# Ten stages of a transformer on one core: each mixer's last slabs taken one at a time, the modulation's column sums in parts or inside the mixers

## The chip, the core and the metric

The kernel runs on one core of a Trainium2 chip. The metric is the device time of one execution in microseconds (us). Before the change it is 3786.5 us, the median of 3 runs (3773.27 to 3791.08). TensorE is called PE below, its weight loads PEld, VectorE DVE, ScalarE ACT, GpSimd POOL and SyncE SP.

## The reference: what is computed

One sequence of 256 tokens with 1024 channels passes two blocks of two layers each. In the first block a layer is a SwiGLU, a mixer and another SwiGLU, each behind an RMS norm that a condition vector modulates. In the second block a layer is a mixer and a mixture of 64 experts of which each token takes 8, modulated in the same way (the text is cut).

```
def adaln_in(x, g, m, i):
    return rmsnorm(x, g) * (1 + m[:, i, 1][:, None]) + m[:, i, 0][:, None]

# first_block, layer l
m = (silu(c) @ w_mod[l] + b_mod[l]).reshape(bsz, 3, 3, D_MODEL)      # shift, scale, gate for 3 parts
x = x + 0.5 * m[:, 0, 2][:, None] * swiglu(adaln_in(x, norm_g[l, 0], m, 0), ffn_w1[l, 0], ffn_w3[l, 0], ffn_w2[l, 0])
h = adaln_in(x, norm_g[l, 1], m, 1) @ w_in[l]
mix = mixer_ab(h, ...) if l % 2 == 0 else mixer_cd(h, ...)
x = x + m[:, 1, 2][:, None] * (mix @ w_out[l])
x = x + 0.5 * m[:, 2, 2][:, None] * swiglu(adaln_in(x, norm_g[l, 2], m, 2), ffn_w1[l, 1], ffn_w3[l, 1], ffn_w2[l, 1])
```

`mixer_ab` joins windowed attention (with a bias from a table) and a gated convolution of three taps. `mixer_cd` joins dense attention and a long convolution by Fourier transform. The second block's mixer joins differential attention, a convolution of 31 taps with a layer norm, and stick-breaking attention; each is projected, gated by a sigmoid and summed, and the sum is projected again.

## The kernel before

**Stages.** The work is cut into ten stages, s = 0 to 9: SwiGLU, mixer ab, SwiGLU (layer 0), SwiGLU, mixer cd, SwiGLU (layer 1), then mixer, experts, mixer, experts. The four instruction streams PE, ACT, DVE and POOL are written out by hand, each as one function with the stages in order; between them there are only semaphore waits, so an engine's order is the order of its program text. x, the residual, stays on chip as eight tiles of 128 channels by 256 tokens. Beside the views, stage 1 runs from about 287 us to 450, stage 3 from 653, stage 4 from 857, stage 6 from 1242, stage 7 from 1639, stage 8 from 2530 and stage 9 from 2892.

**Slabs.** All weights come in slabs of 1 MB. SP issues their loads in the order of use into a ring of six places (for the experts three more, called far); a load waits until the matmuls that read the place before have ended. A mixer's linears use a slab as it is (L990). A SwiGLU and the experts use a split: ACT copies a half slab rounded (hi, L1521, L1528, L1768), DVE subtracts that from it (lo, L2073, L2077, L2587), and PE makes three matmuls from hi and lo of both sides (L895 to L897). `first_halves` splits the first half slabs of a stage. DVE calls it before it adds the last products of the stage before; where a stage is marked `early`, ACT has done its copies at the end of the stage before too.

**Start of a stage.** The last four products of a stage, of two tiles each, are added to x by DVE (L2066, eight instructions). ACT squares each tile (`norm`), PE sums the squares over the channels with a matrix of ones (L876, recorded as 16 instructions), ACT takes the root, DVE the reciprocal, and then DVE scales h and ACT adds the shift, tile by tile (L1511, L1513). ACT loads a table of its functions (L1495) before the first root. For the scale, DVE needs the modulation. In stages 0, 1, 3, 4 and 6 PE makes its column sums (`sum_mods`, L890) just behind the square sums; for stages 2, 5, 7, 8 and 9 they stand in the mixer ahead, before its output projection.

**Modulation.** c is a column of 1024, w_mod of one stage 1024 by 3072. POOL loads w_mod in pieces of 512 KB into two buffers (L813), twelve of them for 1024 columns; DVE multiplies each by its part of silu(c) and adds up in a tile `macc` or in a part of `work` (`add_mods`, L1943 and L1946, 1.3 us each). PE then sums over the partitions: 24 matmuls with one column of ones, which the records show as 48 instructions, into PSUM bank 3. DVE's `take_mods` waits for all 24, adds b_mod, halves the gate where it must and multiplies the gain. In the mixers of stages 6 and 8 `add_mods` is called in three steps by `MIX2_STEPS`: before the heads' norms, before the rotation, and before the convolution's mean is subtracted (L2344), behind which ACT squares (L1592) and PE sums the variance (L1128).

**Mixers of stages 1 and 4.** PE goes through eight query blocks: scores, the transposes of the probabilities (L1020), the product with the values; while it does so it also makes the last input slabs. DVE makes the convolution's tiles in blocks 6 and 7 of stage 1. In stage 4 PE then transforms z, DVE multiplies the spectra (L2273), PE transforms back (L1097), and DVE finishes the product (L2278). Behind that PE runs `sum_mods(s + 1)` and then the output projection.

**Experts.** In stages 7 and 9 a router (L1218) chooses, then PE walks through 64 experts. 49 in each stage are "gathered": a transposed copy of their tokens only (wide or narrow) goes through the three slabs of the expert. For expert n PE runs the first matmuls (L1301 to L1307), turns the rows for the next (L1288), adds the outputs of n - 2 to the tokens (`scatter`, L1349), then runs `finish(n - 1)`, the second matmul of the expert before (L1336, it reads `hidden_few` and also waits for DVE's `hg`, L2606, of a later one), and last `turn_few(n)`, the small transpose of its own hidden rows (L1319) from `pre`, which ACT makes (L1812, L1814). The last matmul of `finish` frees the slab.

**Other work in the way.** `more_setup` (two DMAs on ACT's queue, products and an Exp for the second block's lambda and its tables) stands at the end of stage 0's units on ACT and DVE. At stage 6 ACT waits for all eight tiles of x, issues the DMA of the attention masks and then begins its squares.

## Time and profile before

| what | value |
|---|---|
| median of 3 runs | 3786.5 us (3773.27 to 3791.08) |
| the profiled execution's own time | 3798.87 us |
| its span | 3796.9 us |
| PE busy | 3530.8 us, 93% |
| PE weight loads busy | 2989.7 us, 79% |
| DVE busy | 2332.1 us, 61% |
| ACT busy | 1477.7 us, 39% |
| POOL busy | 240.3 us, 6% |
| DMA moved | 842.63 MB, mean 222 GB/s |

The profile is of one execution. Its span is the time from its first to its last instruction. Busy time is the time in which an engine executes; weight loads lie beside matmuls. A matmul counts as busy while it is in PE's pipeline, so 93% is not 93% of PE's peak.

### The profile page before, as it was taken

What the parts mean: (1) busy time and instruction counts of PE and PEld (TensorE: products, weight loads), DVE (VectorE), ACT (ScalarE), POOL (GpSimd) and SP (SyncE); (2) the same over time, 40 slices, a digit from 0 to 9 for tenths busy, and PEclk for the clock granted to TensorE, in tenths of its full rate; (3) what the DMA queues carried; (4) which work ended last, traced back from release to release, by engine and by line L of the source; (5) the groups of instructions that cost most, each with busy time, mean ns of one, the idle gap of its engine ahead of it and who ended that gap; (6) DMA issues with size and microseconds to landing.
All of it is one profiled execution on the core that took longest, in us unless ns stands there. A gap on an engine that the chain in (4) does not pass through costs nothing.

```text
span 3796.9 us, 52579 instructions
## 1 busy us (share of the span) xinstructions
PE 3530.8 (93%) x21065; PEld 2989.7 (79%) x21065; DVE 2332.1 (61%) x3517; ACT 1477.7 (39%) x2212; POOL 240.3 (6%) x337
## 2 busy tenths in 40 slices
PE   4999899999899998889999999999988999999999
PEld 2997799997699787789767676778778976766776
DVE  6774475775377474546666666656554766666666
ACT  1432233432143204133555555541232355555554
POOL 3010010010001000000000000000000000000000
PEclk9999899999899899889999999999998999999999
DMA  7785286784178552345889998875432688898986
GB/s 260 250 297 165 81 293 196 244 293 152 57 245 303 187 188 100 122 153 183 271 283 292 293 286 283 279 239 171 134 121 90 214 273 270 284 289 274 296 274 191
DMA packets 580320, 842.63 MB, mean 222 GB/s; under 512 B 22715, under 2 KB 489760, under 8 KB 578832
## 3 DMA queue, kind: packets, MB, share of 16 engines
q1 hardware_dynamic: 514508, 665.85, 53.5%
q0 software_dynamic: 41056, 147.35, 11.8%
q10 hardware_dynamic: 24548, 26.57, 2.8%
q8 instruction: 140, 2.29, 0.3%
q14 instruction: 68, 0.56, 0.0%
HBM read 836.37 MB, written 3.33 MB: 221 GB/s over the span
## 4 chain that ended last, share of the span: by engine, by line
PE 77%; DVE 9%; DMA 7%; ACT 3%; issue 2%; SPq 1%; DVEq 0%; ACTq 0%
PE bank L990 14%; PE bank L895 11%; PE bank L896 11%; PE bank L897 11%; PE bank L1336 8%; DMA ring<-in_w 3%; DMA far_up<-in_w 3%; PE bank L1349 2%; PE bank L1306 2%; PE bank L1307 2%; PE bank L1203 2%; PE bank L890 2%; PE bank L1301 2%; PE bank L1303 1%; PE bank L1302 1%
## 5 line engine op out<-in xcount | busy, mean ns | idle before, releaser
L897 PE MATMUL bank<-hh,ring_lo 128*128 128x256 f32 (+1 forms) x2176 | 621.7, 286 | 0.0
L895 PE MATMUL bank<-hh,hi 128*128 128x256 f32 (+1 forms) x1984 | 570.8, 288 | 16.7 <-issue 12.3
L896 PE MATMUL bank<-h_lo,hi 128*128 128x256 f32 (+1 forms) x1984 | 567.0, 286 | 0.0
L990 PE MATMUL bank<-h,ring 128*128 128x256 f32 x2432 | 556.4, 389 | 8.4 <-ACT h L1513 8.4
L990 PEld LDWEIGHTS bank<-h,ring 128*128 128x128 f32 x2432 | 475.7, 196 | 80.2 <-issue 12.1
L897 PEld LDWEIGHTS bank<-hh,ring_lo 128*128 128x128 f32 (+1 forms) x2176 | 419.9, 193 | 0.0
L895 PEld LDWEIGHTS bank<-hh,hi 128*128 128x128 f32 (+1 forms) x1984 | 382.7, 193 | 25.3 <-issue 17.6
L896 PEld LDWEIGHTS bank<-h_lo,hi 128*128 128x128 f32 (+1 forms) x1984 | 382.9, 193 | 0.5 <-issue 0.5
L895 PE MATMUL bank<-hid,hi 128*128 128x256 f32 (+1 forms) x1216 | 346.8, 285 | 2.2 <-DVE ring_lo L2592 2.2
L896 PE MATMUL bank<-hid_lo,hi 128*128 128x256 f32 (+1 forms) x1216 | 343.9, 283 | 0.0
L897 PE MATMUL bank<-hid,ring_lo 128*128 128x256 f32 (+1 forms) x1088 | 307.6, 283 | 0.0
L1521 ACT ACTIVATE hi<-ring 128x1024 fp32r<-128x1024 f32 (+1 forms) x184 | 184.0, 1034 | 284.2 <-DMA ring<-in_ffn_w 138.0
L2073 DVE TENSOR_TENSOR ring_lo<-ring,hi 128x1024 fp32r<-128x1024 f32 (+1 forms) x184 | 213.0, 1195 | 109.6 <-ACT hi L1521 109.6
L1336 PE MATMUL bank<-ring,hidden_few 128*64 128x512 f32 (+1 forms) x512 | 242.2, 618 | 40.3 <-DVE hg L2606 40.0
L2587 DVE TENSOR_TENSOR ring_lo<-ring,hi_far 128x1024 fp32r<-128x1024 f32 x176 | 208.5, 1221 | 59.4 <-ACT hi_far L1768 56.5
L895 PEld LDWEIGHTS bank<-hid,hi 128*128 128x128 f32 (+1 forms) x1216 | 233.0, 192 | 3.5 <-issue 2.5
L896 PEld LDWEIGHTS bank<-hid_lo,hi 128*128 128x128 f32 (+1 forms) x1216 | 233.2, 192 | 0.0
L2587 DVE TENSOR_TENSOR ring_lo<-ring,hi 128x1024 fp32r<-128x1024 f32 x168 | 199.4, 1222 | 45.3 <-ACT hi L1768 39.5
L1946 DVE SCALAR_TENSOR_TENSOR macc<-wmod,cond,macc 128x1024 f32<-128x1024 f32 x126 | 160.8, 1281 | 107.5 <-DMA wmod<-in_w_mod 89.4
L813 POOL DMA_DIRECT2D wmod<-in_w_mod x216 | 114.6, 531 | 1713.2 <-DVE macc L1946 985.9
L897 PEld LDWEIGHTS bank<-hid,ring_lo 128*128 128x128 f32 (+1 forms) x1088 | 208.6, 192 | 0.0
L1336 PEld LDWEIGHTS bank<-ring,hidden_few 128*64 128x64 f32 (+1 forms) x512 | 75.5, 157 | 161.6 <-issue 158.3
(372 smaller groups left out, 6642.6 us busy)
## 6 DMA issues: line engine op xcount, KB each, us to landing
ring<-in_w SPq DMA_DIRECT2D x258, 1024.0 KB, 12.3
ring<-in_ffn_w SPq DMA_DIRECT2D x120, 1024.0 KB, 10.5
wmod<-in_w_mod POOLq DMA_DIRECT2D x216, 512.0 KB, 5.6
far_up<-in_w SPq DMA_DIRECT2D x84, 1024.0 KB, 13.1
ring<-in_w_in SPq DMA_DIRECT2D x74, 1024.0 KB, 6.0
work<-in_w SPq DMA_DIRECT2D x42, 1024.0 KB
ring<-in_w_out SPq DMA_DIRECT2D x16, 1024.0 KB, 5.1
ring<-in_w_mod SPq DMA_DIRECT2D x12, 1024.0 KB, 12.7
```

The costliest lines, as they stand in the source:

```text
L813: pool.dma_start(wmod[:, q % 2, :], w[l][k][:, at:at + D]).then_inc(mod_full[q % 2], 16)
L890: ins = pe.matmul(bank[3][:, j:j + 1], mod_sums(n)[:, j * P:(j + 1) * P], M["ones"][:, 0:1], start=True, stop=True)
L895: pe.matmul(o, w_hi, x_hi, start=start, stop=False, skip_group_check=True)
L896: pe.matmul(o, w_hi, x_lo, start=False, stop=False, skip_group_check=True)
L897: return pe.matmul(o, w_lo, x_hi, start=False, stop=stop, skip_group_check=True)
L990: ins = pe.matmul(o[:, half * T:(half + 1) * T], l_, r_, start=(k == 0), stop=(k == KD - 1))
L1203: ins = pe.matmul(bank[4 + j % 4][:, (m % 2) * T:(m % 2 + 1) * T], w[:, k, m * P:(m + 1) * P], src[:, k, :], start=(k == 0), stop=(k == CT ...
L1336: ins = pe.matmul(bank[2 + half][0:m, :], hidden_few[:, c * m:(c + 1) * m], w[:, c, half * 512:(half + 1) * 512], start=(c == 0), stop=(c ...
L1521: act.activation(up_hi(j, t, m), up_half(slots[j], t, m), ACT.Copy).then_inc(hi_done, 1)
L1946: dve.scalar_tensor_tensor(out=acc, in0=w, scalar=c, in1=acc, op0=ALU.mult, op1=ALU.add).then_inc(mod_step, 1)
L2073: dve.tensor_tensor(up_half(slots[j], t, m, ring_lo), up_half(slots[j], t, m), up_hi(j, t, m), ALU.subtract).then_inc(lo_done, 1)
L2587: dve.tensor_tensor(unit_up(slot, True)[:, j, :, c], unit_up(slot)[:, j, :, c], up_hi(j, t, P, n % 2), ALU.subtract).then_inc(lo_done, 1)
```

## The change: what it does

**Banks.** `sum_mods` becomes `sum_columns` with a choice of columns and bank. At the norms of stages 1, 3, 4 and 6 `sum_first` sums the scale into bank 0, the shift into bank 3 and the gate into bank 1, each with its own count on the semaphore; DVE takes scale and shift before it scales h, the gate after the fourth tile (second in stage 3).

**Mixers.** The sums for stages 2 and 5 move ahead of the last block's transpose of stage 1 (bank 5) and ahead of the inverse transform of stage 4 (bank 7). Those of stage 8, made in stage 6's end before, come at the start of stage 7; those of stage 9 are split over two branch projections of stage 8.

**Ends of mixers.** `end_mixer` replaces `next_halves` and `add_out` on ACT and DVE: first half slab split, four tiles added and squared, other half slabs split, last four tiles. PE sums the first four squares ahead of the last output slab.

**Moves.** `more_setup` goes behind stage 1's norm, the masks' DMA behind that and `load_bias`; the ACT wait at the end of stage 2 is taken out, and in stages 2, 3 and 5 the split of the third slab goes behind the norm. `MIX2_STEPS[8]` becomes 8, 6, 6 (the rest of its pieces is added later, as before). With the experts `turn_few(n)` goes ahead of `finish(n - 1)`, on ACT `turned_few(n)` ahead of `out_hi(n - 1)`, on DVE `out_lo` behind the product; `hidden_few` gets two buffers.

```diff
-        hidden_few = nc.alloc_sbuf_tensor_at("hidden_few", [P, T], F32, offset=place["macc"] + 4 * (2 * D + 2 * T))
+        hidden_few = [nc.alloc_sbuf_tensor_at("hidden_few", [P, T], F32, offset=place["macc"] + 4 * (2 * D + 2 * T)), work[:, 64, :]]
...
+        SHIFT, SCALE, GATE, ALL = range(0, KD), range(KD, 2 * KD), range(2 * KD, 3 * KD), range(0, 3 * KD)
+        SUMS = [("all", 0), ("scale", 1), ("shift", 1), ("gate", 1), ("all", 2), ("scale", 3), ("shift", 3), ("gate", 3),
+                ("scale", 4), ("shift", 4), ("gate", 4), ("all", 5), ("scale", 6), ("shift", 6), ("gate", 6), ("all", 7), ("all", 8), ("all", 9)]
...
-        MIX2_STEPS = {6: (12, 6, 6), 8: (8, 4, 4)}
+        MIX2_STEPS = {6: (12, 6, 6), 8: (8, 6, 6)}
...
+            def norm(s, parts=range(KD)):
...
+                for k in parts:
                     pe.wait_ge(sq_done, KD * s + k + 1)
                     ins = pe.matmul(bank[2][:, 0:T], M["ones"], sq[:, (k + 4) % KD, :], start=(k == 0), stop=(k == KD - 1))
-                ins.then_inc(ms_done, 1)
...
+                if KD - 1 in parts:
+                    ins.then_inc(ms_done, 1)
...
+            def sum_columns(n, columns, to, at=0):
...
+                for i, j in enumerate(columns):
+                    ins = pe.matmul(bank[to][:, at + i:at + i + 1], mod_sums(n)[:, j * P:(j + 1) * P], M["ones"][:, 0:1], start=True, stop=True)
+                return ins
+
+            def sum_mods(n, to=3):
...
-                for j in range(MODT):
-                    ins = pe.matmul(bank[3][:, j:j + 1], mod_sums(n)[:, j * P:(j + 1) * P], M["ones"][:, 0:1], start=True, stop=True)
-                ins.then_inc(mod_summed, 1)
+                sum_columns(n, ALL, to).then_inc(mod_summed, 1)
...
+            def sum_first(n):
...
+                pe.wait_ge(mod_step, MOD_STEPS * n)
+                sum_columns(n, SCALE, 0).then_inc(mod_summed, 1)
+                sum_columns(n, SHIFT, 3).then_inc(mod_summed, 1)
+                sum_columns(n, GATE, 1).then_inc(mod_summed, 1)
...
                         linear(slabs[6 + i // 2], 6 + i // 2, taken0, halves=(i % 2,))
+                    if i == 7 and sec["kind"] == "ab":
+                        pe.wait_ge(proj_taken, taken0 + 6)
+                        sum_mods(s + 1, 5)
                     turn_probs(X, i, probs(i))
                     value(i)
                 if sec["kind"] == "cd":
...
                 pe.wait_ge(*X("o_taken", 4))
-                sum_mods(s + 1)
                 pe.wait_ge(*X("conv", CT))
                 for c in range(4):
                     linear(slabs[9 + c], 9 + c, taken0, heads=att)
...
+                    if c == 2:
+                        norm(s + 1, range(4))
...
                     ins.then_inc(X["uf"], 1)
+                sum_mods(s + 1, 7)
                 pe.wait_ge(*X("prod", 4))
...
+                        if (br_, half) == (1, 1) and s == 8:
+                            pe.wait_ge(*X("o_taken", 8))
+                            pe.wait_ge(mod_step, MOD_STEPS * 9)
+                            sum_columns(9, range(0, MODT // 2), 3)
+                        if (br_, half) == (2, 0) and s == 8:
+                            sum_columns(9, range(MODT // 2, MODT), 3, MODT // 2).then_inc(mod_summed, 1)
...
-                sum_mods(8 if s == 6 else 9)
...
                 for c in range(4):
                     linear(slabs[34 + c], 40 + c, taken0)
+                    if c == 2:
+                        norm(s + 1, range(4))
...
+                        turn_few(n)
                         finish(n - 1)
-                        turn_few(n)
...
-                norm(sec["s"])
-                if sec["s"] in (0, 1, 3, 4, 6):
-                    sum_mods(sec["s"])
+                norm(sec["s"], range(4, KD) if sec["behind_mixer"] else range(KD))
+                if sec["s"] in (0, 7):
+                    sum_mods(0 if sec["s"] == 0 else 8)
+                if sec["s"] in (1, 3, 4, 6):
...
+                if not sec["behind_mixer"]:
+                    act.activation(idle, eps, ACT.Sqrt)
+                    squares(s, range(KD))
...
+                if sec["kind"] == "ffn" and sec["early"]:
+                    first_halves(sec, 2)
...
+            def end_mixer(sec):
...
+                act.activation(idle, eps, ACT.Sqrt)
+                split_up(slots[0:1], 0, lambda j: counts[0], m)
+                squares(s, range(4))
+                act.wait_ge(full[slots[1]], counts[1])
+                act.activation(up_hi(1, 0, m), up_half(slots[1], 0, m), ACT.Copy).then_inc(hi_done, 1)
+                first_halves(nxt, 1)
+                if nxt["kind"] == "moe":
+                    first_halves(nxt, 2)
+                squares(s, range(4, KD))
...
-                        act.wait_ge(down_done, tile + 3)
                         first_halves(plan[sec["s"] + 1], 1)
...
+                        turned_few(n)
                         out_hi(n - 1)
-                        turned_few(n)
...
-                if s == 6:
-                    act.wait_ge(x_done, KD * (s + 1))
-                    act.dma_start(masks.rearrange("p a t -> p (a t)"), A["k_causal"]).then_inc(masks_in, 16)
                 norm(sec)
                 if s == 1:
+                    more_setup()
                     load_bias()
+                    act.dma_start(masks.rearrange("p a t -> p (a t)"), A["k_causal"]).then_inc(masks_in, 16)
                 if s == 6:
...
-                dve.wait_ge(mod_summed, s + 1)
-                then(dve.tensor_tensor(m[:, :], bank[3][:, 0:MODT], vec[:, bg, ba:ba + MODT], ALU.add))
-                if s < 6 and s % 3 != 1:
+                m, first, end = modc[:, n % 3, :], columns[0], columns[-1] + 1
+                if what is not None:
+                    dve.wait_ge(*sums(*what))
+                then(dve.tensor_tensor(m[:, first:end], bank[b][:, at:at + end - first], vec[:, bg, ba + first:ba + end], ALU.add))
+                if n < 6 and n % 3 != 1 and end == 3 * KD:
                     then(dve.tensor_scalar(m[:, 2 * KD:], m[:, 2 * KD:], 0.5, None, ALU.mult))
-                then(dve.scalar_tensor_tensor(out=gain[:, s % 3, :], in0=m[:, KD:2 * KD], scalar=1.0, in1=vec[:, gg, ga + row * KD:ga + (row + 1) * KD],
-                                              op0=ALU.add, op1=ALU.mult))
+                if first <= KD < end:
+                    then(dve.scalar_tensor_tensor(out=gain[:, n % 3, :], in0=m[:, KD:2 * KD], scalar=1.0, in1=vec[:, gg, ga + row * KD:ga + (row + 1) * KD],
+                                                  op0=ALU.add, op1=ALU.mult))
...
-                if s not in (7, 8):
-                    take_mods(s)
+                if s == 0:
+                    take_mods(0, ("all", 0), 3)
+                if s in (1, 3, 4, 6):
+                    take_mods(s, ("scale", s), 0, 0, SCALE)
+                    take_mods(s, ("shift", s), 3, 0, SHIFT)
                 dve.wait_ge(rstd_done, s + 1)
                 for k in range(KD):
                     dve.scalar_tensor_tensor(out=h[:, k, :], in0=x[:, k, :], scalar=gain[:, s % 3, k:k + 1], in1=rstd[:, :], op0=ALU.mult, op1=ALU.mult).then_inc(scaled_done, 1)
+                    if s in (1, 3, 4, 6) and k == (1 if s == 3 else 3):
+                        take_mods(s, ("gate", s), 1, 0, GATE)
...
+                    if sec["early"]:
+                        first_halves(sec, 2)
...
                         conv_tile(2 * (i - 6))
+                        if i == 7:
+                            take_mods(s + 1, ("all", s + 1), 5)
                         conv_tile(2 * (i - 6) + 1)
...
+                    take_mods(s + 1, ("all", s + 1), 7)
                     for t in range(CT):
...
+                lo_up(slots[0:1], 0, lambda i: counts[0][0], m)
+                add_out(0)
+                add_out(1)
+                dve.wait_ge(hi_done, counts[0][1])
+                dve.tensor_tensor(up_half(slots[1], 0, m, ring_lo), up_half(slots[1], 0, m), up_hi(1, 0, m), ALU.subtract).then_inc(lo_done, 1)
+                first_halves(nxt, 1)
+                if nxt["kind"] == "moe":
+                    first_halves(nxt, 2)
+                add_out(2)
+                add_out(3)
...
-                        out_lo(n - 1)
                         spread_slots(n)
                         if slots(n) == NARROW:
                             dve.wait_ge(product_done, g0 + p + 1)
-                            dve.tensor_tensor(hidden_few[:, 0:P], product[:, 0:P], bank[1][:, P:2 * P], ALU.mult).then_inc(hid_done, 2)
+                            dve.tensor_tensor(hidden_few[p % 2][:, 0:P], product[:, 0:P], bank[1][:, P:2 * P], ALU.mult).then_inc(hid_done, 2)
+                        out_lo(n - 1)
...
                 norm(sec)
+                if s == 1:
+                    more_setup()
...
                 if sec["kind"] == "moe":
+                    if s == 7:
+                        take_mods(8, ("all", 8), 3)
```

## Rows read from the trace of the kernel before

**Rows 1.** The page, the chain that ended last: shares of the span by engine.

```profile
PE 77%; DVE 9%; DMA 7%; ACT 3%; issue 2%; SPq 1%; DVEq 0%; ACTq 0%
```

**Rows 2.** Timeline, stage 1's start (start us, duration us, engine, line, operation; [idle before, releaser]).

```profile
284.66 3.22 DVE L2066 SCALAR_TENSOR_TENSOR x<-bank,modc,x 128x256 f32<-128x256 f32 x8 [1.98 <-PE bank L897]
...
295.60 5.92 PE L890 MATMUL bank<-mats,work 128*128 128x1 f32 x48
...
303.15 1.19 PE L990 MATMUL bank<-h,ring 128*128 128x256 f32 x2 [1.63 <-ACT h L1513]
...
334.73 3.35 DVE L2175 RECIPROCAL work<-work 128x512 f32<-128x512 f32 x1 [12.38 <-ACT work L1599]
```

**Rows 3.** Timeline, stage 4's start.

```profile
854.66 3.22 DVE L2066 SCALAR_TENSOR_TENSOR x<-bank,modc,x 128x256 f32<-128x256 f32 x8 [1.98 <-PE bank L897]
...
860.08 7.09 PE L890 MATMUL bank<-mats,work 128*128 128x1 f32 x48
...
868.79 1.62 PE L990 MATMUL bank<-h,ring 128*128 128x256 f32 x3 [1.63 <-ACT h L1513]
```

**Rows 4.** Timeline, stage 3's start.

```profile
648.73 1.58 ACT L1521 ACTIVATE hi<-ring 128x768 fp32r<-128x768 f32 x2 [2.50 <-PE bank L897]
...
657.02 5.58 PE L890 MATMUL bank<-mats,macc 128*128 128x1 f32 x48
...
664.91 0.50 PE L895 MATMUL bank<-hh,hi 128*96 128x256 f32 x1 [2.31 <-issue]
```

**Rows 5.** Timeline, stage 6's start.

```profile
1239.61 3.23 DVE L2066 SCALAR_TENSOR_TENSOR x<-bank,modc,x 128x256 f32<-128x256 f32 x8 [1.98 <-PE bank L897]
...
1243.26 1.28 ACT L1495 ACT_TABLE_LOAD   x1 [6.87 <-DVE x L2066]
...
1260.15 1.19 PE L990 MATMUL bank<-h,ring 128*128 128x256 f32 x2 [1.63 <-ACT h L1513]
```

**Rows 6.** Timeline, end of the mixer of stage 1.

```profile
405.77 1.12 PE L1020 MATMUL bank<-mats,pb 128*128 128x128 f32 x4 [2.95 <-DVE pb L2233]
...
410.12 10.40 PE L890 MATMUL bank<-mats,macc 128*128 128x1 f32 x48 [0.47 <-ACT work L1642]
```

**Rows 7.** Timeline, end of the mixer of stage 4.

```profile
991.85 9.53 PE L1097 MATMUL bank<-work 128*128 128x256 f32 x32 [8.39 <-DVE work L2273]
...
1001.21 8.17 PE L890 MATMUL bank<-mats,macc 128*128 128x1 f32 x48
...
1002.77 0.42 DVE L2278 TENSOR_TENSOR h<-work 128x256 f32<-128x256 f32 x1
```

**Rows 8.** Timeline, start of stage 2: the square sums.

```profile
451.21 3.72 PE L876 MATMUL bank<-pb,mats 128*128 128x256 f32 x16 [1.57 <-ACT pb L1499]
```

**Rows 9.** Timeline, end of stage 6 and start of stage 7.

```profile
1602.72 5.76 PE L890 MATMUL bank<-mats,macc 128*128 128x1 f32 x48
...
1646.19 1.09 PE L1218 MATMUL bank<-wr,h 128*128 128x64 f32 x4 [3.51 <-ACT h L1513]
```

**Rows 10.** Timeline, around the layer norm of stages 6 and 8.

```profile
1423.11 2.53 DVE L1946 SCALAR_TENSOR_TENSOR macc<-wmod,cond,macc 128x1024 f32<-128x1024 f32 x2 [4.30 <-DMA wmod<-in_w_mod]
...
1428.12 3.78 PE L1128 MATMUL bank<-work,mats 128*128 128x256 f32 x8 [4.75 <-ACT work L1592]
...
2690.71 1.06 ACT L1592 ACTIVATE work<-work 128x1024 f32<-128x1024 f32 x1 [5.59 <-DVE work L2344]
...
2692.95 1.89 PE L1128 MATMUL bank<-work,mats 128*128 128x256 f32 x8
```

**Rows 11.** Expert stages: a wait (us, times, longest), a chain row, two timeline rows.

```profile
PE bank L1336 <- DVE hg L2606: 50.9, 34, 3.0
...
2216.12 13.05 DMA ring<-in_w
...
2180.09 0.58 ACT L1814 ACTIVATE pre<-bank 128x512 f32<-128x512 f32 x1
...
2181.80 1.10 PE L1319 MATMUL bank<-sort,pre 128*128 128x64 f32 x8
```

95 lines of the change are left out of this document (44 added, 51 removed).

## The prediction

> **What bounds the kernel now.** I read the page first: the shares, then the chain that ended last. TensorE (PE) is 77% of that chain, so a microsecond is won only where PE stands still or does work that could lie in a standstill [rows 1]. Then I took the timeline at the start of every stage (stage s is the code's section s, 0 to 9), at the ends of the four mixers, and the waits of the two expert stages (7 and 9), and asked at each spot which wait ends last. Three kinds show up. At a stage's start PE sums squares, then makes 48 one-column matmuls for the modulation, and only then does the vector engine (DVE) form h: those 48 take 5.6 to 7.1 us there [rows 2 to 4]. At the end of mixers 1 and 4 the same 48 stand between the last attention or convolution work and the output projection, 10.4 and 8.2 us, just behind PE waits [rows 6, 7]. In the expert stages PE waits 50.9 us in 34 places for DVE's hg in front of an expert's second matmul [rows 11].
>
> **Order at stage starts (stages 1, 3, 6).** Stage 4 is the pattern with nothing in the way: first add to x at 854.66, square sums over at 860.08, 5.4 us later, first slab at 868.79, 14.1 us later [rows 3]. In stage 1 the set-up that the diff moves makes this 10.9 us (284.66 to 295.60) [rows 2]: gain 5.5. What it issues (two DMAs, some fifteen small DVE operations, an Exp on ScalarE (ACT) and its table, with one table change back) now lies behind the norm of stage 1, where DVE later waits 12.38 us for ACT's roots while PE runs its first slabs [rows 2]; without that cover it costs about 4 us. In stage 6 ACT waited 6.87 us, until all eight tiles were added, then issued the mask DMA and loaded its table at 1243.26, and only then squared; first add to first slab takes 20.5 us (1239.61 to 1260.15) [rows 5]. By stage 4's 14.1 us the order is worth 6.4. In stage 3 ACT waits 2.50 us for PE before it splits the next slab's second half [rows 4]; with the wait gone and the third slab's split behind the norm, DVE's adds can begin when the sums are there. I take 2.1 of the 2.50.
>
> **Three banks at the norms (stages 1, 3, 4, 6).** Now DVE waits for all 48, then needs three or four operations and ACT one before PE starts: in stage 1 PE starts its slab 7.55 us after the square sums (295.60 to 303.15), of which 5.92 are the 48 [rows 2]; in stage 4 8.71, of which 7.09 [rows 3]; in stage 3 7.89, of which 5.58 [rows 4]. After the change DVE goes on when two thirds are done, and the gate's third runs beside it; but PE is in order, so its slab can't start before all 48 are done. New starts: 5.92 and 7.09 us behind the square sums, so 1.6 us won in each of stages 1 and 4; in stage 3 both paths end near 5.5, so 2.3. And h is then ahead of PE's first half slab, which today gets one tile per 0.4 us: estimate 0.9 more in stages 1, 4 and 6, after the gate's own two small DVE operations are paid. Stage 6 as stage 4 then takes 5.4 + 7.1 = 12.5 us from add to slab, 12.6 with the wait's own cost, so 7.9 less than its 20.5, and 0.9. Totals: stage 1 8.0, stage 3 4.4, stage 4 2.5, stage 6 8.8. The least is the order alone (5.5, 2.1 and 6.4, so 14.0), the most also has the sums at 5.6 us each (3 more).
>
> **Sums into the mixers.** Mixer 1: the 48 move in front of the last transpose, where PE waited 2.95 us; today they take 10.40 at its end [rows 6]. The work is the same, so only the wait is filled: gain 3.0. Behind the new PE operation are the last transpose and value product; DVE's wait for it stands ahead of the last convolution tile, which ends before PE is through. Mixer 4: they go in front of the inverse transform, where PE waits 8.39 us; they took 8.17 [rows 7], so they fit. What is late next: DVE's last product of the convolution, ending at 1003.19 (1002.77 plus 0.42), which the sums hid; PE can then start at about 1003.3 instead of 1009.24: gain 6.0. Below: 3 if the sums slow the matmuls behind; above: 8 with 2.4 GHz throughout.
>
> By the Trainium skill (TensorE: Matmul & The Clock Gate, "The HAM clock gate") activity releases the throttle, so sums laid into waits should run at 2.4 GHz and win more. The trace doesn't bear this out for one-column matmuls: those issued back to back at 410.12 took 10.40 us, those at 1602.72 5.76 [rows 6, 9]. By the page mixer 1 would win 7.6 instead of 3.0, and the whole would come to 3748.
>
> **Slab by slab (stages 2, 5, 7, 9).** In stage 2 DVE did no add before the third slab was split, so all eight adds and squares came behind PE's last slab: PE stood 1.57 us, then made the square sums in 3.72 [rows 8], over 5.3 us after that slab. New: four square sums (half of 3.72, so 1.86) stand in front of it, and behind it remain two adds, two squares and two sums, about 2.0 us: gain 1.4. DVE no longer takes the modulation behind the reciprocal: 0.5 more. Stage 5 repeats stage 2: 4.0 for both. In stages 7 and 9 PE had no wait there; four sums move from behind the slab to ahead of it, between a loss and a gain of one sum pair (0.5), and I take 0. In stage 7 the modulation's 5.76 us [rows 9] leave PE's path to the projection and fall into the 3.51 us that PE waits for h before the router where 2.3 stick out; 0.4 goes to the modulation's DVE operations: gain 3.1. Stage 9's 48 are put between two projections where PE is busy: 0.
>
> **Earlier mod steps in stage 8.** The counts go from 8, 4, 4 to 8, 6, 6. Each step waits for its own 512 KB DMA through two buffers. Two more before the rotation: about 1.6 us of DVE, and the tap chain behind it shifts. Two more before the mean is subtracted: stage 6, which has six there, shows them: the last two came after 4.30 us of waiting and took 2.53, 6.8 together, PE's variance matmul stood idle 4.75 us and took 3.78 us instead of 1.89 [rows 10]. In stage 8 PE had no wait there (2692.95), and ACT's squares were done at 2691.77, 1.2 us before [rows 10]. So 1.6 plus 6.8 minus 1.2 plus about 1.1 for slower matmuls (half of stage 6's excess of 1.9): a loss of 8.3. What it removes (four steps beside projections, no PE wait) wins nothing. Bounds: loss of 4 to 11.
>
> **Experts: the transpose ahead of the second matmul.** Per gathered expert the small transpose (1.10 us for a narrow one [rows 11], 0.4 for a wide one) goes ahead of the previous expert's second matmul, into the hg wait. Counted place by place, each wait filled by at most the transpose, this gives about 29 us over the 98 experts. Against it: the transpose waits for pre, which ACT makes after splitting a slab that may just be landing. At 2180.09 it makes pre while PE is already in the second matmul; PE would have stood 2.5 us there [rows 11]. Such places and small ones of 0.1 to 0.4 sum to some 11 us. And the second matmul's end frees the slab whose loads take 13.05 us on the chain [rows 11]. Counted from the end of one such matmul to another, both orders have the same number of transposes, so a chain that runs over slab loads gets no shorter; only waits inside DVE and ACT count. Ends: minus 11 and plus 29; I take 3, nearest to the chain.
>
> **The sum.** 8.0 + 4.4 + 2.5 + 8.8 + 3.0 + 6.0 + 4.0 + 3.1 - 8.3 + 3.0 = 34.5 us. Against the profiled execution (3798.87 us, span 3796.9) that is 3764.4; that execution is 12.4 above the median of the runs, 3786.5, so I forecast 3752.
>
> **Rivals.**
> *The experts' waits are really filled.* If DVE and ACT, not loads, set the hg waits, the 29 count in full: 3752 - 26 = 3726. For it: the waits end on DVE. Against: behind DVE stand ACT and a 13 us load on the chain. Chance 0.13.
> *Only the orders count.* If PE's in-order queue takes back what the split sums and the mixers' sums fill, there remain 14.0 at three starts, 4.0 in stages 2 and 5, minus 8.3: gain 9.7, 3777. For it: filled waits bring PE no less work. Against: 8.39 us of idle PE with 8.17 us of work to put in. Chance 0.20.
> *Slower: later releases.* Each second matmul of the experts now ends later by the transpose, 66 by 1.1 and 32 by 0.4, 85 us in all. If the loads are what bounds stages 7 and 9, and the transposes don't get ahead of their waits, every delay is passed to a load: 31.5 - 85, so 54 us slower, 3840. It decides from about 40% of these delays on. For it: loads of 13 us on the chain. Against: the same number of transposes on a path between two releases. Chance 0.07.
> The forecast has 0.60, its own range 3740 to 3765.
>
> **Range and chances.** From just under the first rival to the second: 3728 to 3778. A measurement of this kernel tells about 0.5% from no change, 19 us, so from 3767.6 down it is faster: the forecast, the first rival and a little of the second, 0.76; within, 0.17; slower 0.07.
>
> **What would show it.** Right: square sums of stages 1 and 6 end 5.4 us after the first add; stage 1's set-up stands behind its norm without PE waiting; no 48 sums ahead of mixer 1's and 4's projections, and a PE wait of about 2 us for DVE there in mixer 4; in stage 8 a PE wait of 5 to 7 us before the variance matmul and later tap chain; in the experts PE's idle for hg down but new idle for pre, and stages 7 and 9 within 5 us of before. Wrong: hg waits gone and the expert stages over 10 us shorter; no wait in stage 8; or the expert stages longer with loads landing later.

## The result, and the profile after

The changed kernel takes 3742.28 us (median of 4 runs, 3736.55 to 3747.96), the kernel before 3779.92 in the same comparison; the ratio is 0.9893, 95% interval 0.9871 to 0.9915. In a second comparison of the same two programs it is 3740.68 against 3787.87, ratio 0.9868 (0.9848 to 0.9888). So it is faster by 38 us in the one and 47 in the other; 34.5 were forecast. The profiled execution has a span of 3741.5 us, against 3796.9 before, 55.4 less. That pair seems to overstate the gain: the execution of before shown ahead of the prediction took 3798.87 us, where the medians of before are 3779.92 to 3791.28 in the four comparisons (but 3800.03 for the same program as b_again, below).

The page of the changed kernel: span, busy times, chain that ended last.

```profile
span 3741.5 us, 52688 instructions
PE 3523.4 (94%) x21065; PEld 2988.2 (80%) x21065; DVE 2328.0 (62%) x3525; ACT 1464.8 (39%) x2213; POOL 246.2 (7%) x337
PE 75%; DVE 11%; DMA 8%; ACT 4%; issue 2%; SPq 1%; DVEq 0%; ACTq 0%
```

PE is busy for 7.4 us less and idle for 48 less, and DVE's and DMA's share of the chain is up [rows 1]: the gain is PE idle time. Where it was shows a window for each stage, from its first weight matmul to that of the next (stage 9: to PE's last). First the changed kernel, then a second profile of the kernel before. Columns: stretch, length, then busy us (instructions) of PE, PEld, DVE, ACT, POOL; granted clock of PE (1.00 is 2.4 GHz, 0.50 is 1.2), DMA share, GB/s. Length less PE busy is PE's idle time.

```profile
93.33:295.57 202.24, 202.24 (x1648) 201.82 (x1649) 148.00 (x192) 79.72 (x105) 19.01 (x36) 0.98 0.78 268
295.57:447.42 151.85, 139.78 (x632) 119.80 (x632) 64.24 (x138) 38.98 (x91) 6.41 (x12) 0.91 0.40 131
447.42:650.48 203.06, 202.03 (x1649) 201.56 (x1649) 140.06 (x187) 82.64 (x108) 12.66 (x24) 0.98 0.70 237
650.48:852.51 202.03, 202.03 (x1649) 201.61 (x1649) 148.93 (x193) 80.62 (x106) 19.00 (x36) 0.98 0.77 265
852.51:1024.28 171.77, 151.16 (x661) 124.06 (x662) 84.46 (x149) 35.94 (x82) 6.33 (x12) 0.92 0.32 103
1024.28:1226.20 201.92, 201.92 (x1648) 201.50 (x1649) 148.84 (x193) 80.52 (x106) 19.01 (x36) 0.98 0.80 273
1226.20:1605.34 379.14, 346.18 (x1542) 294.71 (x1542) 210.92 (x395) 91.42 (x159) 17.94 (x34) 0.95 0.43 145
1605.34:2486.80 881.46, 847.54 (x5005) 665.97 (x5006) 562.40 (x816) 438.03 (x643) 53.25 (x51) 0.98 0.84 267
2486.80:2859.80 373.00, 341.24 (x1492) 288.68 (x1493) 191.79 (x371) 86.74 (x152) 12.76 (x24) 0.95 0.40 133
2859.80:3737.09 877.29, 845.15 (x5004) 663.54 (x5004) 562.11 (x818) 434.78 (x635) 48.82 (x49) 0.99 0.82 261
```

```profile
99.73:308.06 208.33, 202.83 (x1649) 201.77 (x1649) 149.01 (x209) 79.49 (x105) 19.00 (x36) 0.98 0.77 261
308.06:464.31 156.25, 139.33 (x630) 118.95 (x631) 63.12 (x121) 38.24 (x92) 6.41 (x12) 0.90 0.41 132
464.31:669.84 205.53, 201.32 (x1648) 200.61 (x1649) 139.73 (x185) 82.85 (x108) 12.67 (x24) 0.98 0.68 227
669.84:873.72 203.88, 202.25 (x1648) 201.78 (x1649) 147.14 (x190) 78.81 (x103) 19.01 (x36) 0.98 0.78 263
873.72:1054.26 180.54, 152.47 (x660) 125.16 (x661) 85.73 (x151) 37.88 (x86) 6.34 (x12) 0.90 0.34 106
1054.26:1265.14 210.88, 205.86 (x1648) 204.69 (x1649) 147.14 (x190) 77.83 (x103) 19.01 (x36) 0.96 0.76 257
1265.14:1648.85 383.71, 351.46 (x1541) 298.30 (x1541) 209.54 (x393) 90.58 (x157) 17.94 (x34) 0.93 0.43 143
1648.85:2538.09 889.24, 845.39 (x5004) 663.67 (x5005) 567.91 (x819) 446.80 (x648) 50.16 (x51) 0.98 0.83 265
2538.09:2893.96 355.87, 330.99 (x1493) 283.38 (x1493) 191.36 (x371) 86.87 (x152) 12.76 (x24) 0.97 0.43 139
2893.96:3783.43 889.47, 846.11 (x5004) 664.90 (x5004) 565.81 (x818) 440.60 (x635) 45.24 (x49) 0.98 0.81 257
```

Stages 0, 3 and 5 now have no idle PE at all from one first slab to the next: length and busy time are equal. Stage 8 is the one that became longer. The timeline of the changed kernel at the starts of stages 1 and 6 and at the sums of stages 3 and 4, which answers to [rows 2 to 5]:

```profile
282.55 3.23 DVE L2119 SCALAR_TENSOR_TENSOR x<-bank,modc,x 128x256 f32<-128x256 f32 x8 [1.97 <-PE bank L914]
287.96 7.75 PE L891 MATMUL bank<-mats,work 128*128 128x1 f32 x48
295.57 1.20 PE L1007 MATMUL bank<-h,ring 128*128 128x256 f32 x2
...
642.30 7.15 PE L891 MATMUL bank<-mats,macc 128*128 128x1 f32 x48
...
846.26 6.39 PE L891 MATMUL bank<-mats,work 128*128 128x1 f32 x48
...
1213.76 3.23 DVE L2119 SCALAR_TENSOR_TENSOR x<-bank,modc,x 128x256 f32<-128x256 f32 x8 [1.98 <-PE bank L914]
1219.17 7.17 PE L891 MATMUL bank<-mats,work 128*128 128x1 f32 x48
1226.20 2.05 PE L1007 MATMUL bank<-h,ring 128*128 128x256 f32 x4
```

At the starts of stages 1 and 6 the sums begin 5.4 us after the first add, and the first slab starts when they end, with no wait. Stage 1's now take 7.75 us instead of 5.92, stage 3's 7.15 instead of 5.58, stage 4's 6.39 instead of 7.09. The mixers, stage 8's layer norm and the projection of stage 6, answering to [rows 6, 7, 9, 10]:

```profile
395.40 10.24 PE L891 MATMUL bank<-mats,macc 128*128 128x1 f32 x48
...
975.43 4.97 PE L1119 MATMUL bank<-work 128*128 128x256 f32 x11 [1.11 <-DVE work L2329]
...
986.87 3.62 PE L1007 MATMUL bank<-work,ring 128*128 128x256 f32 x8 [1.93 <-issue]
...
1566.51 22.67 PE L1007 MATMUL bank<-h,ring 128*128 128x256 f32 x96 [1.96 <-DVE h L2513]
...
2648.09 3.78 PE L1150 MATMUL bank<-work,mats 128*128 128x256 f32 x8 [5.58 <-ACT work L1641]
```

Mixer 4's wait of 8.39 us is down to 1.11. Before its output projection a new wait of 1.93 us stands: the profile names no releaser, but DVE's last product of the convolution ends at 986.77, 0.1 us before the projection starts, as the prediction had it. The projection of stage 6, which followed the sums, now waits 1.96 us for the merged h. Stage 8's variance matmul waits 5.58 us and takes 3.78 instead of 1.89. And PE's waits in the experts, answering to [rows 11] (us in total, times, longest), first of the changed kernel, then of the changed kernel with the old order of the experts (a_noswap, below):

```profile
PE bank L1366 <- DVE hg L2674: 14.2, 23, 0.9
PE bank L1349 <- ACT pre L1863: 8.6, 10, 3.0
PE bank L1345 <- DVE product L2710: 5.7, 14, 0.7
```

```profile
PE bank L1366 <- DVE hg L2674: 51.7, 33, 3.6
```

### The profile page after: what moved, and what is told of

Same layout as the page of the kernel before. It is cut to its first block, busy times and chain, and to the rows that moved or that the text cites. A ratio compares the mean times of both kernels' runs of the same rounds, so it can differ in the third digit from the quotient of the medians.

```text
span 3741.5 us, 52688 instructions
## 1 busy us (share of the span) xinstructions
PE 3523.4 (94%) x21065; PEld 2988.2 (80%) x21065; DVE 2328.0 (62%) x3525; ACT 1464.8 (39%) x2213; POOL 246.2 (7%) x337
## 3 DMA queue, kind: packets, MB, share of 16 engines
q0 software_dynamic: 41056, 147.35, 11.7%
## 4 chain that ended last, share of the span: by engine, by line
PE 75%; DVE 11%; DMA 8%; ACT 4%; issue 2%; SPq 1%; DVEq 0%; ACTq 0%
PE bank L1007 12%; PE bank L912 11%; PE bank L914 11%; PE bank L913 11%; PE bank L1366 8%; DMA ring<-in_w 3%; DMA far_up<-in_w 3%; DVE work L2400 2%; PE bank L1335 2%; PE bank L1379 2%; PE bank L1336 2%; PE bank L1231 2%; PE bank L1330 2%; PE bank L891 1%; PE bank L1331 1%
## 5 line engine op out<-in xcount | busy, mean ns | idle before, releaser
L1559 ACT ACTIVATE hi<-ring 128x1024 fp32r<-128x1024 f32 (+1 forms) x180 | 180.5, 1035 | 110.2 <-DMA ring<-in_ffn_w 84.4
L795 POOL DMA_INDIRECT got<-rows_scratch,slot_tok x98 | 98.5, 1005 | 1700.4 <-PE bank L1317 1258.2
L1817 ACT ACTIVATE hi_far<-ring 128x1024 fp32r<-128x1024 f32 x176 | 178.2, 1057 | 66.1 <-DMA ring<-in_w 66.1
## 6 DMA issues: line engine op xcount, KB each, us to landing
ring<-in_w_mod SPq DMA_DIRECT2D x12, 1024.0 KB, 12.1
```

What stands on the lines that cost most here:

```text
L795: pool.indirect_dma_start(got[0:m, p % 2, :], None, rows_dram[l].ap(), bass.IndirectOffsetOnAxis(slot_tok[0:m, rank - WIDE_FROM:rank - WID ...
L1559: act.activation(up_hi(j, t, m), up_half(slots[j], t, m), ACT.Copy).then_inc(hi_done, 1)
L1817: act.activation(up_hi(j, t, P, n % 2), unit_up(slot)[:, j, :, t * P:(t + 1) * P], ACT.Copy).then_inc(hi_done, 1)
```

## The experiments

All ratios are to the kernel before, of the same comparison.

**b_again**: no edit.

> The kernel before, unchanged. The two profiled executions differ by 55.4 us, the medians by 37.6, so either the profiled execution of before was a long one (its 3798.87 us against a median of 3780) or the changed one a short one. If the first, this profile has a span near 3780 and its stages 7 and 9 (first matmul to first matmul 891.3 and about 898 us before) are shorter by most of the difference, since DMA is what varies; the PE wait for hg in them is then nearer 40 us than the 50.9 of before. If the waits are the kernel's own, hg stays at 51 us within 2. The ratio shows what the measurement can tell: 1.000 within 0.003.

3800.03 us, ratio 1.0013 (0.9996 to 1.0031); span 3787.8. Stages 7 and 9 together have 1778.7 us against 1784.7 in the first profile, stage 8 355.9 against 361.7, stages 0 to 5 the same within 0.1. The first profile was long by 11.8 us in these three stages. The hg waits are 46.9 us, between the two expectations. That DMA is what varies is not shown: the 5.8 us of stage 8 are all PE busy time (336.8 against 331.0, at a granted clock of 0.96 and 0.97), and of the 6.0 in stages 7 and 9 only 4.2 are PE idle time.

**b_swap** and **a_noswap**: the experts' order alone, and everything but it.

```diff
-                        finish(n - 1)
-                        turn_few(n)
+                        turn_few(n)
+                        finish(n - 1)
```
(ACT and DVE likewise; b_swap has two `hidden_few` too.)

> The kernel before with the experts' order alone: the small transpose ahead of the second matmul, two buffers for the hidden rows, the outputs' splits behind. My forecast (loads set the pace, the filled waits come back elsewhere): 3 us faster, within 5. The rival (PE sets the pace, what the waits lose is won): 20 to 29 us faster, as the profiled pair has it: stages 7 and 9 shorter by 26 us there with hg waits 36.7 us less and 14.3 us of new waits for pre and product. If the pair overstates it by the long execution of before, about 10 to 18.

> The changed kernel with the experts' three orders put back (PE, ACT and DVE; the second buffer stays). By my forecast 3 us slower than the changed kernel, 3745; by the rival 20 to 29 us slower, 3762 to 3771, with hg waits of PE back at about 50 us. With the kernel before with the swap alone it tells whether the gain is additive.

b_swap: 3777.89 us, ratio 0.9958 (0.9940 to 0.9977), so 16 us faster. a_noswap: 3758.89, ratio 0.9918 (0.9903 to 0.9933), 9 us more than the changed kernel's 0.9893 in the first comparison and 19 more than its 0.9868 in the second. The lengths of stages 7 and 9 together, in all profiles but that of a_pre844:

```
old order: 1784.7 1778.7 1781.6 1782.5                              mean 1781.9, PE idle 89.7
new order: 1773.7 1758.8 1767.1 1770.0 1768.5 1773.1 1771.7 1760.4 1772.0   mean 1768.4, PE idle 69.5
```

The two sets don't overlap; the swap is worth 13.5 us. PE idles 20.2 us less, and 6.7 of them come back as longer PE busy time. My forecast of 3 is wrong, and the rival's 20 to 29 is too high: 29 is twice what came. The 16 us of b_swap, whose profile stands for one execution only, fit the third expectation, 10 to 18.

**b_orders**: `more_setup` and the masks' DMA moved, nothing else.

```diff
-                if s == 6:
-                    act.wait_ge(x_done, KD * (s + 1))
-                    act.dma_start(masks...)
                 norm(sec)
                 if s == 1:
+                    more_setup()
                     load_bias()
+                    act.dma_start(masks...)
```
(`more_setup` is taken from the end of stage 0 on both engines; DVE calls it behind stage 1's norm likewise.)

> The kernel before with two moves alone: more_setup behind stage 1's norm, the masks' DMA behind stage 1's norm instead of ahead of stage 6's squares. Forecast by the prediction's terms: stage 0 to the first slab of stage 1 5.5 us shorter (208.3 to 202.8), stage 5 to the first slab of stage 6 6.4 shorter (210.9 to 204.5), nothing lost in stage 1 (156.2): 11.9 us in all, 0.9969. Rival: the moved set-up holds DVE and ACT where the queries' norms need them, stage 1 is 2 to 4 us longer.

3777.45 us, ratio 0.9961 (0.9945 to 0.9978): 15 us, where 11.9 were forecast. The profiled execution was the longest of 13, and its granted clock was lower in most stages (0.93 in stages 0, 3 and 5 where others have 0.98; 0.90 in stage 8), so its windows of stages 0, 1 and 5 are read with care:

```profile
97.79:301.92 204.13, 202.50 (x1649) 201.93 (x1649) 147.76 (x190) 78.60 (x103) 19.01 (x36) 0.93 0.78 266
301.92:462.47 160.55, 143.82 (x630) 120.41 (x631) 65.36 (x140) 40.91 (x95) 6.43 (x12) 0.87 0.41 131
1049.87:1253.38 203.51, 201.88 (x1649) 201.32 (x1649) 147.20 (x190) 78.59 (x103) 19.01 (x36) 0.93 0.78 265
```

Even so stages 0 and 5 are 4.2 and 7.4 us shorter than before (5.5 and 6.4 were forecast). Stage 1 is 4.3 longer, but its idle time (length less busy) is 16.7 us against 16.9 before: PE's busy time is 4.5 longer at 0.87, and the moved set-up added no wait. The rival falls.

**a_again**: the changed kernel a second time.

> The changed kernel, unchanged, beside the others of this call: the base from which they are read. The profiles so far have stages 0 to 5 of the changed kernel within 1 us of each other but for stage 1 (146.1, 150.9 and 151.9 us), and the expert stages spread over 13 us and more for one and the same order. Expected: ratio to before 0.988 to 0.991, stages 7 and 9 together near 1770 us, between the 1760.4 of the first profile and the 1773.3 of the kernel with 8, 4, 4. If the first profile's 1760.4 comes again, the experts' order is worth over 20 us; if 1770 and more, about 10.

3740.68 us, ratio 0.9868. Stages 7 and 9: 1767.1. Stage 1 took 146.1 us instead of 151.9 with the same program.

**a_wait48**: DVE waits for the gate's sums, the last third, before scale and shift.

```diff
-                    take_mods(s, ("scale", s), 0, 0, SCALE)
-                    take_mods(s, ("shift", s), 3, 0, SHIFT)
+                    take_mods(s, ("gate", s), 0, 0, SCALE)
+                    take_mods(s, ("gate", s), 3, 0, SHIFT)
```

> The changed kernel, but DVE waits for all 48 column sums at the norms of stages 1, 3, 4 and 6 before it takes scale and shift; banks and PE's order stay. By the prediction's terms the split wait is worth 2.5, 2.3, 2.5 and 2.4 us there, 9.7 in all, which would come back: 3752. The rival after the first comparison: stage 0 gained 6.1 us of which the order alone explains 5.5, so the split wait is worth about 0.6 in stages 1 and 6 and the sums themselves have become longer (7.75 us instead of 5.92 in stage 1): 2 to 5 us come back.

3757.02 us, ratio 0.9905 (0.9884 to 0.9926), 14 us more than a_again. Its windows of stages 0, 2, 3 and 5:

```profile
97.72:301.85 204.13, 202.32 (x1649) 201.84 (x1649) 147.22 (x191) 78.80 (x103) 19.08 (x36) 0.98 0.78 266
453.01:657.72 204.71, 202.28 (x1648) 201.81 (x1649) 140.23 (x187) 82.77 (x108) 12.72 (x24) 0.98 0.70 235
657.72:861.83 204.11, 202.30 (x1649) 201.82 (x1649) 148.46 (x192) 79.70 (x104) 19.08 (x36) 0.98 0.78 263
1035.11:1239.11 204.00, 202.19 (x1648) 201.71 (x1649) 148.57 (x192) 79.62 (x104) 19.08 (x36) 0.98 0.79 270
```

They are 2.0, 1.8, 2.1 and 2.1 us longer than in a_again, 8.0 together, and 1.8, 1.4, 1.8 and 1.8 of it is new PE idle time. So the split wait is worth 8.0 where the prediction had 9.7; the rival's 2 to 5 is refuted. The other 6 of the 14 us I can't place: in the profile stage 1 is 5.1 us longer too, but all of that is PE busy time at a lower clock (0.92 against 0.95), which differs between executions of one program.

**a_oldends**: the mixers' ends in the old order.

```diff
-                    if c == 2:
-                        norm(s + 1, range(4))
...
+                first_halves(nxt, 0)
+                first_halves(nxt, 1)
+                act.activation(idle, eps, ACT.Sqrt)
+                squares(s, range(KD))
```

> The changed kernel with the ends of the mixers as before: all half slabs of the next stage split first, then the eight adds, all squares and square sums behind the last slab. By the prediction 4.0 us slower, 2.0 each at the starts of stages 2 and 5 (stage 1 and stage 4 longer by that) and nothing in 7 and 9. Rival: the early square sums also help stages 7 and 9, by 1 to 2 us each, because PE then waits for the last squares there, or they hurt by delaying the last slab's products.

3743.00 us, ratio 0.9862 (0.9838 to 0.9886) against 0.9868: no difference, but an interval of 9 us to either side could not show 4. The windows of stages 1 and 4 can:

```profile
300.07:445.64 145.57, 133.67 (x631) 114.67 (x632) 64.14 (x138) 38.93 (x91) 6.40 (x12) 0.95 0.43 139
850.35:1021.64 171.29, 149.98 (x662) 122.08 (x662) 84.44 (x149) 35.89 (x82) 6.33 (x12) 0.91 0.34 106
```

0.5 and 0.8 us shorter than in a_again. Both expectations are wrong for these stages. From the end of stage 1's last slab to the first matmul of stage 2 the old order takes 7.6 us (438.05 to 445.64) and the changed kernel 6.3 (441.12 to 447.42), but that one has made four square sums in 1.7 us ahead of the slab. Before it was 9.9 (449.5 to 459.35). Of the 2.3 us between before and the old order 0.4 are the modulation, which DVE no longer takes behind the reciprocal (in a_mixback, where it does, the gap is 6.75 us instead of 6.30). Most of the rest is PE's wait for the first squares, 1.57 us in before and none in a_oldends. In before DVE began its adds at 450.23, when it had split the third slab (1.22 us from 449.09; ACT's copy for it had waited for the slab's load); in both later kernels that split stands behind the norm. No run moves the split alone.

**a_mixback**: sums for stages 2 and 5 back at the mixers' ends.

```diff
                 pe.wait_ge(*X("o_taken", 4))
+                sum_mods(s + 1)
                 pe.wait_ge(*X("conv", CT))
```
(and out of their new places; DVE takes them behind the reciprocal.)

> The changed kernel with the sums for stages 2 and 5 back at the ends of the mixers of stages 1 and 4. By the prediction 9.0 us slower (3.0 in stage 1, 6.0 in stage 4): stage 1 at 149 to 155 us, stage 4 at 178. The whole gain of stages 1 and 4 over before (4.3 to 10.1 and 7.5 to 8.7) must then be of these moves, since the old ends cost nothing. Rival: part of it comes from the modulation no longer being taken behind the reciprocal (0.5 us each) and from the clock, which stands at 1.2 GHz during the sums in some executions and at 2.4 in others; then stage 1 comes out anywhere between 146 and 156.

3767.63 us, ratio 0.9936 (0.9915 to 0.9957), 26 us more than a_again, and 16 more than the changed kernel's first comparison; its profile, against a_again's, shows 17 us in stages 1 and 4:

```profile
301.60:457.66 156.06, 139.34 (x632) 119.24 (x632) 64.00 (x138) 38.96 (x91) 6.41 (x12) 0.92 0.40 128
862.95:1042.06 179.11, 152.69 (x661) 125.27 (x662) 84.38 (x149) 36.07 (x83) 6.34 (x12) 0.90 0.32 99
```

Stage 4 is 7.0 us longer than in a_again (172.1), stage 1 10.0 longer, or 4.2 against the first profile's 151.9. The idle time doesn't vary so: in stage 1 it is 16.7 us here and 12.1 in both profiles of the changed kernel, so 4.6 us are filled waits. They are the wait ahead of the last transpose, which is 4.21 us here (2.95 in before, where the clock was lower and PE came there later), and the 0.4 us of the modulation. What stage 1 gains beyond that, from nothing to 5.3 us, is PE busy time and hangs on the clock. The rest of the 26 lies in stages 7 to 9 and the spread of runs, and I don't assign it.

**a_844 and a_844_2**: stage 8's steps put back.

```diff
-        MIX2_STEPS = {6: (12, 6, 6), 8: (8, 6, 6)}
+        MIX2_STEPS = {6: (12, 6, 6), 8: (8, 4, 4)}
```

> The changed kernel with stage 8's steps at 8, 4, 4 again. Stage 8 took 11.3 us more in the changed kernel, with a PE wait of 5.58 us before the variance matmul and 3.78 instead of 1.89 us for it. Forecast: those go, 8 to 11 us faster than the changed kernel, 3732 to 3735. Rival: the steps are needed, because the sums for stage 9 now stand between two branch projections and wait for the last step: four more steps come behind the value products, a new PE wait of 3 to 6 us stands before these sums, and the gain is under 5 us.

> The changed kernel with 8, 4, 4 a second time, as the base of this call. Its first profile had stage 8 at 361.5 us against 367.6 to 373.0 in the profiles with 8, 6, 6, so I expect 6 to 11 us less than the changed kernel (ratio to before 0.984 to 0.987). If the ratio is 0.988 or more, the shorter stage 8 is given back in the run as a whole.

3743.42 us, ratio 0.9871 (0.9844 to 0.9899), and 3729.34, ratio 0.9856 (0.9834 to 0.9878); mean 0.9864 against 0.9881 for the changed kernel: 6 us, which the intervals don't separate. The profile does. Stage 8 of the second:

```profile
2479.83:2838.43 358.60, 331.75 (x1493) 283.23 (x1493) 191.69 (x371) 86.82 (x152) 12.80 (x24) 0.97 0.42 138
```

In four profiles with 8, 4, 4 it takes 358.4 to 361.5 us (mean 359.5), in six with 8, 6, 6 367.6 to 373.0 (mean 370.9). The wait before the variance matmul is gone and no wait stands before stage 9's sums: the rival falls, the steps cost 11.4 us, of which 5.6 are PE idle time (32.5 against 26.8) and 5.8 PE busy time. This is the version with the lowest median, though its interval doesn't part it from the changed kernel.

**a_late844**: 8, 4, 4, and stage 1's sums between output slabs two and three.

```diff
                     linear(slabs[9 + c], 9 + c, taken0, heads=att)
+                    if c == 1 and sec["kind"] == "ab":
+                        sum_mods(s + 1)
```
(and out of their place ahead of the last transpose; DVE takes them before its last adds.)

> The changed kernel with 8, 4, 4 and stage 1's sums between the second and the third slab of its output projection, where PE has been busy at 2.4 GHz. There 24 columns took 2.73 us in stage 8, so 5.5 for the 48 against 6.3 or 10.2 ahead of the last transpose; the PE wait of 2 us there is no longer filled. Expected: stage 1 at 146 to 148 us in every execution, 0 to 4 us faster than 8, 4, 4 alone. Rival: the sums at the clock's low level hide behind DVE's last operations in the mixer, and stage 1 gets 2 us longer.

3741.06 us, ratio 0.9875 (0.9854 to 0.9896), 7 us more than a_844_2, which the intervals don't part. The sums took 5.86 us, but stage 1 153.85 us, above all of the 145.6 to 152.3 with the sums ahead of the last transpose: PE's idle time there is 15.6 us instead of 12.1. In this one profile the rival is right: the wait that is no longer filled (3.5 us) costs more than the better clock under the sums wins.

**a_pre844**: 8, 4, 4, and ACT makes pre ahead of the next expert's first split.

```diff
-                        split_ups(n + 1, 0)
                         middle(n)
+                        split_ups(n + 1, 0)
```

> The changed kernel with 8, 4, 4 where ACT makes pre of an expert before it splits the first half slabs of the next. PE's new waits for pre (8.6 to 14.4 us in the profiles of the changed order) are those in which ACT sits in a split of a slab that has just landed. If that is their cause they go to under 3 us, and the expert stages get up to 10 us shorter. Rival: the splits come later by ACT's wait for the first matmuls, PE's waits for the lo halves in front of the next expert grow by more, and the stages get longer.

4013.28 us, ratio 1.0590 (1.0573 to 1.0606), 284 us slower than a_844_2 in the same comparison. PE's largest waits, and the window of stage 7:

```profile
PE bank L1345 <- DVE product L2710: 97.4, 32, 3.7
PE bank L1366 <- DVE hg L2674: 97.2, 51, 3.5
```

```profile
1602.52:2627.73 1025.21, 896.76 (x5006) 684.43 (x5006) 553.84 (x816) 435.80 (x644) 49.10 (x51) 0.93 0.74 229
```

PE no longer waits for pre, so the cause of those waits was the one named. But the split now starts after PE's first matmuls, DVE's lo half comes after that, and product and hg, which DVE makes behind it, after that: 194.6 us of these waits, where a_844_2 had 19.2, for 11.7 of pre removed; and a lower clock on top (0.93; PE busy 48.8 us more than in a_844_2). The waits for the lo halves in front of the next expert grew too, from 15.2 us to 42.1, by more than the 11.7 removed, as the rival said; but most of the loss stands behind them, where I had not looked.

## Why the prediction was right, and where not

Predicted and measured, the latter as the mean of the two profiles of before less that of the two of the changed kernel:

| step | predicted | measured |
|---|---|---|
| start of stage 1 (order, three banks) | 8.0 | 6.1 (208.3 to 202.2) |
| start of stage 3 | 4.4 | 2.6 (205.6 to 203.0) |
| start of stage 4 | 2.5 | 1.9 (203.9 to 202.0) |
| start of stage 6 | 8.8 | 9.0 (210.9 to 201.9) |
| mixer 1, start of stage 2 | 3.0 + 2.0 | 7.2 (4.4 and 10.1) |
| mixer 4, start of stage 5 | 6.0 + 2.0 | 8.6 (180.5 to 171.9) |
| stage 6's end, start of stage 7 | 3.1 | 7.8 (384.9 to 377.1) |
| stage 8 | -8.3 | -11.5 (358.8 to 370.3) |
| experts | 3.0 | 13.5 over all profiles (18.8 in these four) |
| sum | 34.5 | 45.2 |

**Starts.** Right in mechanism. Where PE can no longer wait, the stage ends at its own busy time, 202 us, and what I estimated beyond that (0.9 for h being ahead of the first half slab) did not show: PE's own order of work sets the start. And the sums became longer at a lower clock: stage 1's 7.75 us at 0.68 instead of 5.92 at 0.90, stage 3's 7.15 at 0.74 instead of 5.58 at 0.96. By a_wait48 the split wait gave 2.0 in stage 1 (2.5 predicted), 1.8 in stage 3 (2.3) and 2.1 in stage 6, so the orders gave 4.1 (5.5), 0.8 (2.1) and 6.9 (6.4), and b_orders alone gave 4.2 and 7.4 in stages 1 and 6. The miss is the length of the sums, which I held constant: without the split wait PE's idle time before stage 3 still fell by 1.8 us (from 4.2 to 2.4 in a_wait48), about what I had taken, but the sums took 7.42 us there, 1.8 more than before; in b_orders stage 1's took 7.36, 1.4 more.

**Mixers.** Mixer 4 as predicted, 7.0 by a_mixback (6.0 and 0.5 for the modulation); the PE wait left before the inverse transform is 1.11 us, and the wait for DVE's last product that I had named came, 1.93 us. Mixer 1: the wait was filled as predicted, and the filling is worth 4.6 us of idle time by a_mixback where I had 3.5; the rest of its gain, or none, comes with the clock, see below.

**Slab by slab.** The step failed. "Behind it remain two adds, two squares and two sums" is true, but the four sums ahead are PE work too, and PE is what bounds. A gain of 3.9 us was there (from the last slab's end to the next stage's first matmul, with the four sums counted in: 9.9 to 8.0 us in stage 2, 10.1 to 8.0 in stage 5), so the number came out right for a wrong reason. 0.9 of it is the modulation, as predicted. The rest fits the third slab's split behind the norm, a part of the change that I had counted in stage 3 alone; a_oldends shows that it isn't the slab-by-slab order.

**Stage 8.** Right in mechanism, and too low: 11.4 by the profiles with 8, 4, 4 for the steps. The wait (5.58 and 6.03 us) was inside the 5 to 7 us forecast and the variance matmul longer by its full 1.89, where I had put about 1.1 (and half of stage 6's excess is 0.95). The other 3.9 us are longer PE busy time in the rest of the stage, at a granted clock of 0.94 to 0.96 instead of 0.97 and 0.98; the prediction had no term for it.

**Stage 6's end.** The 3.51 us before the router went, 1.96 appeared before the projection, and PE's idle time over the stage fell only from 32.7 us to 32.0 (means of two). The gain is in PE's busy time, 352.2 to 345.1, at a granted clock of 0.95 and 0.96 instead of 0.93. So 3.1 was right for neither reason nor size; why the clock stands higher is open.

**Experts.** The step that failed most. I wrote that "a chain that runs over slab loads gets no shorter", and took 3 of a range from -11 to 29. Loads did not bound: with the old order PE stood idle 90 us of 1782 and was busy in the rest, so the idle time in front of one engine's operation was the kernel's own. The second matmuls now stand behind the transposes and free their slabs that much later, and the stages got shorter all the same. PE's sum of waits for hg, pre and product fell from 51.7 us in a_noswap to 28.5 in the changed kernel's profile (28.5 to 36.9 in the nine with the new order), and the two stages are 13.5 us shorter for it. The sign that I had named as wrong, expert stages over 10 us shorter with the hg waits gone, is what came. The count by place (29 filled, 11 lost by a late pre: 18) was the better forecast; the "nearest to the chain" choice threw it away. Of the rivals, "the waits are really filled" was half right, "only the orders count" and "slower: later releases" fell.

The total is 3 us off by the first comparison and 13 by the second. The misses were 10.5 too little at the experts, 4.7 in stage 6 and 2.8 in the mixers, against 4.1 too much at the starts and 3.2 in stage 8. That the time came out so near is in part luck: misses of 18.0 and 7.3 us stand against each other, and the terms of 3.1 and 4.0 were paid in the main by something else than what I had named. One slip stands in the rival by the Trainium skill: with 7.6 instead of 3.0 for mixer 1 the whole comes to 3747, not 3748.

## What to carry to other kernels

Look at the idle time of the busiest engine by stage first: where length equals its busy time nothing more is to be had from order, and where the idle time in front of its own operations makes up the rest, filling it with work that it must do anyway pays: in the expert stages here two thirds of the idle time that went. Work moved ahead of a spot on an in-order engine pays only if that engine stood still there; four sums moved from behind a slab to ahead of it paid nothing here. A producer's copy that looks early may be holding up three things behind it on the next engine: ask what stands behind before it is put second.

## What the runs showed of the hardware

The same 48 one-column matmuls took 5.58 us at a granted clock of 0.96 (stage 3, before), 7.15 at 0.74 (stage 3, after) and 10.24 at 0.50 (mixer 1). In mixer 1 two executions of the same program differ; windows over the sums, first in the first profile of the changed kernel, then in a_again (columns as above):

```profile
395.40:405.50 10.10, 10.10 (x49) 10.10 (x48) 5.34 (x15) 0.00 (x0) 0.00 (x0) 0.50 0.11 42
```

```profile
397.70:400.00 2.30, 2.30 (x23) 2.27 (x22) 2.16 (x6) 0.00 (x0) 0.00 (x0) 1.00 0.71 210
400.00:404.00 4.00, 4.00 (x30) 4.00 (x30) 3.72 (x12) 0.00 (x0) 0.00 (x0) 0.76 0.04 14
```

The clock had fallen to 1.2 GHz before the sums began in the one (0.66 over the 3.4 us ahead of them, 1.00 in the other), and in their midst in the other; ahead of both stand the same PE waits of 1.96 and 0.69 us. The stage took 151.9 and 146.1 us. In eight profiles with the sums at this place they took 10.24 us four times and 6.2 to 6.4 four times, with nothing between. Why the clock falls earlier in one execution than in another stays open. The rule weighed in the prediction (the Trainium skill, TensorE: Matmul & The Clock Gate, "The HAM clock gate"), that activity releases the throttle, did not help them: PE worked back to back through 10.1 us at 0.50. The clock came back in the first output slab, whose first eight matmuls took 3.78 us and the next eight 1.98.
